# State-space branch stepped by four tokens with matrix powers, and the masks of a stick-breaking head issued as a group

## The chip, the cores and the metric

The kernel runs on one NeuronCore of one Trainium2 chip. The metric is the device time of one execution in microseconds (us). Engines: PE (TensorE, matrix products; PEld are its weight loads), DVE (VectorE), ACT (ScalarE), POOL (GpSimd), SP (SyncE, which here only issues DMAs).

## The reference, cut to what matters

Two transformer blocks follow each other on a sequence of 512 tokens (plus 256 context or memory tokens). The change is in the mixer of the second block, which has three branches on one projection: stick-breaking attention (8 heads of 64), a causal convolution, and a state-space model of 16 groups with 64 complex states each, 16 inputs and 16 outputs per group (1024 complex states in all). The first and the third are these:

```python
z = einsum('bhqd,bhkd->bhqk', qb, kh) * scale
mask = key_pos[None, :] < q_pos[:, None]
log_1mb = where(mask, log_sigmoid(-z), 0.0)
later = cumsum(log_1mb, axis=3, reverse=True) - log_1mb
w = where(mask, exp(log_sigmoid(z) + later), 0.0)
out = einsum('bhqk,bhkd->bhqd', w, vh)
...
# a = exp(lambda dt), |a| = mag;  b~ = f * b
bu = einsum('blgh,gph->blgp', u, bbr), einsum(..., bbi)
x[l] = a * x[l-1] + bu[l]              # complex, by an associative scan
y[l] = Re(c x[l]) + d * u[l]
o_ssm = (y @ glu_w)[:, :256] * sigmoid((y @ glu_w)[:, 256:])
```

The three branches are normed, joined and multiplied with the output weights (`w_out`).

## The kernel before, in words

Activations lie transposed: channels on the 128 partitions, tokens on the free axis. Every large product runs over a stream of 307 weight tiles of 128 x 1024 (`PLAN`; SP loads them into `RAW`, ACT rounds the high part into `HL`, POOL subtracts it for the low part, line 568, and PE multiplies three pairs). `T_OUT2` is the first tile of the second block's `w_out`, `T_U2` the first of its input projection. The order of the work is written out by hand, engine by engine; semaphores tie the engines together.

Between the last tile of the key and value projections of the memory and tile `T_OUT2` no weight tile is multiplied. This stretch, called the head loop here, is the stage that the change is in. PE first turns the state-space input weights (line 1194), multiplies the first half of the convolution's pointwise product (`conv_point(0)`, line 1142), then `state_in(0)` (line 1173), and then runs `stick(h)` for the eight heads:

- for the key blocks i = 3, 2, 1, 0 a score product (line 1209: 64 rows of the array, 128, 256, 384 and 512 columns) and behind each of them a mask product that adds a large negative value on the diagonal block (line 1210: 128 rows, 128 columns). ACT takes |z| of each bank (line 1822), then one exp and one ln over all four (lines 1825, 1827); DVE adds max(z, 0) (line 2759, tile `SPB`).
- meanwhile PE does `state_in(h + 1)` (2 products of 512 columns), then `values(h - 1)` of the head before (line 1235; in head 0 `conv_point(1)` stands here).
- the ten cumulative-sum products on `SPB` (line 1222), whose results ACT turns into weights (line 1833), and last `state_out(h - 1)` (line 1183, 2 products of 512 columns).

The eight state chunks c hold 128 complex states each. In `turn_in` DVE turns the input by the phase of each token within a 128-token segment (tables `TC`, `TS_`), `state` runs the scan with the real factor `mag`: four segments, one behind the other, with the last value turned and carried over (lines 2724, 2729, 2731), and `turn_out` (lines 2737 to 2741) turns back. `state_y` adds `d * u`. `discretize` (lines 2616 to 2622) multiplies the input weights with f before PE turns them. In head 0 ACT also rounds the first three `w_out` tiles (line 1368), and the third waits until POOL has freed a `RAW` buffer and SP has refilled it. Earlier, POOL makes the phase tables between the tiles from `T_TURNS` on (line 623). `PE`, `ACT`, `DVE` each follow their own list, so an instruction that waits holds all behind it on its engine.

After the heads the branches are normed (`mix_...`), the gated product is made (line 1261), and `w_out` starts (line 728).

## Time and profile before

| | us |
|---|---|
| median of 3 runs (2536.8 to 2538.82) | 2537.65 |
| the profiled execution, whole | 2538.42 |
| its span, first to last instruction | 2536.6 |
| head loop, first pointwise product to last values product | 1810.30 to 1944.13 |
| PE busy over the span | 2432.7 (96%) |
| DVE / ACT / POOL busy | 1420.1 / 912.8 / 1048.4 |

The page gives the busy time of each engine, forty slices of the span and the chain of work that ended last. Busy shares over the whole span say little on a stage of 134 us; the stage is read from the chain of waits, from the timeline (instructions in order of time) and from the busy times of chosen windows.

### The profile page before, as it was taken

The page shows a single profiled execution, that of the slowest core. Times are in us where ns is not written, and L with a number is a line of the kernel's source. Part 1 is how long each engine was busy: PE and PEld are TensorE (multiplying, and loading weights), DVE is VectorE, ACT ScalarE, POOL GpSimd, SP SyncE. Part 2 cuts the span into 40 slices and gives each one's busy share as a digit, 9 for nine tenths or more (in the row PEclk, how much of TensorE's full clock was granted, in tenths as well). Part 3 has the DMA queues.
Part 4 walks back from the last instruction along what each step waited for, and adds up shares of the span by engine and source line. Part 5 has one row for each costly group of instructions (what it writes and reads, how often), then busy time and mean ns, then how long its engine had stood idle before and what let it go on. Part 6 is the DMA issues. An engine that isn't in the chain of part 4 may idle for free.

```text
span 2536.6 us, 32104 instructions
## 1 busy us (share of the span) xinstructions
PE 2432.7 (96%) x12008; PEld 2063.8 (81%) x12008; DVE 1420.1 (56%) x2012; ACT 912.8 (36%) x1436; POOL 1048.4 (41%) x815
## 2 busy tenths in 40 slices
PE   6999889999999999999999999999899999999999
PEld 5899789999999998766788888778554766788887
DVE  7747866746465644889542123455788433543433
ACT  4222333313131224778542233345334343322322
POOL 1523132535344422298644467445400332344444
PEclk8999999999999999999999999999899999999999
DMA  6424012323333331411223322233200221232323
GB/s 245 147 100 141 27 58 79 138 100 117 117 108 117 105 111 43 123 39 44 79 84 99 100 92 86 89 108 108 100 1 1 67 67 50 83 100 92 100 91 108
DMA packets 68855, 232.24 MB, mean 92 GB/s; under 512 B 8048, under 2 KB 10992, under 8 KB 68592
## 3 DMA queue, kind: packets, MB, share of 16 engines
q1 hardware_dynamic: 68720, 230.35, 27.4%
q8 instruction: 95, 1.56, 0.3%
q14 instruction: 40, 0.33, 0.0%
HBM read 219.57 MB, written 2.10 MB: 87 GB/s over the span
## 4 chain that ended last, share of the span: by engine, by line
PE 76%; issue 7%; DVE 7%; POOL 6%; ACT 2%; DMA 1%; SPq 1%; POOLq 0%; DVEq 0%; ACTq 0%
PE PS L710 55%; PE PS L728 8%; POOL HL L568 4%; PE PS L751 2%; PE PS L1222 1%; POOL XR L610 1%; PE PS L1209 1%; DVE RD L2530 1%; POOL PL L610 1%; SPq L467 1%; PE PS L1325 1%; DMA EARLY<-adastream 1%; PE PS L1235 1%; DVE OG L2344 1%; PE PS L1173 1%
## 5 line engine op out<-in xcount | busy, mean ns | idle before, releaser
L568 POOL TENSOR_TENSOR HL<-RAW,HL 128x512 fp32r<-128x512 f32 x614 | 873.6, 1445 | 1361.8 <-ACT HL L1368 1361.6
L710 PE MATMUL PS<-HID,HL 128*128 128x384 f32 (+1 forms) x2832 | 562.1, 359 | 1.0 <-DVE HID L2086 1.0
L710 PE MATMUL PS<-HA,HL 128*128 128x512 f32 (+2 forms) x2592 | 553.1, 365 | 8.7 <-DVE VA L2453 2.3
L710 PEld LDWEIGHTS PS<-HID,HL 128*128 128x128 f32 x2832 | 509.5, 188 | 51.8 <-DVE HID L2086 1.4
L710 PE MATMUL PS<-HB,HL 128*128 128x512 f32 (+2 forms) x2592 | 538.7, 359 | 0.0
L710 PEld LDWEIGHTS PS<-HA,HL 128*128 128x128 f32 x2592 | 465.4, 189 | 74.2 <-issue 22.5
L710 PEld LDWEIGHTS PS<-HB,HL 128*128 128x128 f32 x2592 | 462.8, 188 | 50.6
L1368 ACT ACTIVATE HL<-RAW 128x1024 fp32r<-128x1024 f32 x307 | 323.2, 1053 | 476.0 <-PE PS L710 386.2
L2142 DVE CUSTOM_DVE_ANT_0 ADJ<-ADA,CB 128x1024 f32<-128x1024 f32 x160 | 262.3, 1640 | 12.0 <-DVE X L2062 5.2
L2062 DVE SCALAR_TENSOR_TENSOR X<-PS,MOD,X 128x256 f32<-128x256 f32 (+1 forms) x160 | 80.7, 546 | 288.7 <-PE PS L710 274.4
L2091 DVE TENSOR_TENSOR T<-T 128x768 f32<-128x768 f32 (+1 forms) x64 | 73.4, 1148 | 198.5 <-ACT T L1429 198.2
L728 PE MATMUL PS<-HA,HL 128*128 128x384 f32 (+1 forms) x576 | 126.9, 376 | 13.7 <-DVE HA L2032 6.2
L1429 ACT ACTIVATE T<-PS 128x384 f32<-128x384 f32 (+1 forms) x96 | 46.8, 522 | 241.0 <-PE PS L710 164.9
L728 PEld LDWEIGHTS PS<-HA,HL 128*128 128x128 f32 x576 | 107.3, 195 | 31.0 <-issue 10.8
L728 PE MATMUL PS<-HB,HL 128*128 128x384 f32 (+1 forms) x576 | 121.6, 367 | 6.5 <-DVE HB L2788 4.4
L728 PEld LDWEIGHTS PS<-HB,HL 128*128 128x128 f32 x576 | 105.4, 191 | 19.6 <-DVE HB L2788 4.8
L1385 ACT ACTIVATE T<-X 128x512 f32<-128x512 f32 (+2 forms) x64 | 43.6, 684 | 209.6 <-issue 73.5
L2060 DVE TENSOR_TENSOR X<-PS,X 128x512 f32<-128x512 f32 x40 | 27.7, 691 | 147.3 <-PE PS L710 135.3
L610 POOL TENSOR_TENSOR XR<-X,XR 128x512 fp32r<-128x512 f32 x64 | 81.6, 1292 | 24.6 <-ACT XR L1695 24.4
L2086 DVE TENSOR_TENSOR HID<-T,HID 128x768 fp32r<-128x768 f32 (+1 forms) x64 | 75.3, 1176 | 2.6 <-DVE T L2091 0.4
L2903 DVE RECIPROCAL T<-T 128x512 f32<-128x512 f32 x22 | 73.8, 3353 | 0.8
L2901 DVE TENSOR_SCALAR T<-T 128x512 f32<-128x512 f32 x22 | 10.4, 474 | 102.7 <-ACT T L1951 102.7
(409 smaller groups left out, 2647.1 us busy)
## 6 DMA issues: line engine op xcount, KB each, us to landing
RAW<-wstream SPq DMA_DIRECT2D x307, 512.0 KB, 3.4
ADA<-adastream SPq DMA_DIRECT2D x80, 512.0 KB, 3.4
EARLY<-adastream SPq DMA_DIRECT2D x16, 512.0 KB, 14.6
QB<-QH SPq DMA_DIRECT2D x32, 128.0 KB, 2.3
X<-x_in SPq DMA_DIRECT2D x8, 384.0 KB, 6.6
QC<-QL SPq DMA_DIRECT2D x16, 128.0 KB, 2.3
out<-X SPq DMA_DIRECT2D x8, 256.0 KB, 2.2
X<-mem SPq DMA_DIRECT2D x1, 1024.0 KB, 5.7
```

The lines of the kernel that those rows point to most:

```text
L568: a = pool.tensor_tensor(HL[:, t % RING, 1, half], RAW[:, t % RAW_RING, half], HL[:, t % RING, 0, half].bitcast(F32), ALU.subtract)
L610: pool.tensor_tensor(rest, full, high.bitcast(F32), ALU.subtract).then_inc(S("att_prob"), 1)
L710: mm = pe.matmul(PS[:, bk, 0:hi - lo], w[:, wp, k * P:(k + 1) * P], a[:, ap, lo:hi], start=(k == 0 and (wp, ap) == (0, 0)), stop=(k == nk ...
L728: mm = pe.matmul(PS[:, bk, 0:hi - lo], HL[:, tt % RING, wp, k * P:(k + 1) * P], a[:, ap, lo:hi], start=(k == order[0] and (wp, ap) == (0, 0)),
L751: mm = pe.matmul(PS[:, bk, 0:width], H(k)[:, ap, b * P:(b + 1) * P], HL[:, t % RING, wp, kk * width:(kk + 1) * width], start=(k == 0 and ( ...
L1368: act.activation(HL[:, t % RING, 0, :], RAW[:, t % RAW_RING, :], ACT.Copy).then_inc(S("w_hi"), 1)
L1429: a = act.activation(T1[:, j % 2, lo:hi], PS[:, bk, 0:hi - lo], ACT.Relu)
L2062: a = dve.scalar_tensor_tensor(X[:, m, p:q], src, MOD[:, gate[0], gate[1] * KC + m, c:c + 1], X[:, m, p:q], ALU.mult, ALU.add)
L2086: dve.tensor_tensor(HID[:, j, 1, lo:hi], T2[:, j % 2, lo:hi], HID[:, j, 0, lo:hi].bitcast(F32), ALU.subtract).then_inc(S("hid_ready"), 1)
L2091: dve.tensor_tensor(T2[:, j % 2, lo:hi], T1[:, j % 2, lo:hi], T1[:, j % 2, lo:hi], ALU.mult).then_inc(S("hid_v"), 1)
L2142: dve.tensor_tensor_reduce(ADJ[:, :], tile, CB[:, v, :], 1.0, 0.0, ALU.mult, ALU.add, dst).then_inc(S("ada_done"), 1)
L2903: dve.reciprocal(T1[:, j % 2, x], T1[:, j % 2, x]).then_inc(S("ffn_step"), 1)
```

## The change

The state-space branch steps by four tokens. Tokens are dealt into four streams: token 4j + i goes to stream i, column j. `UU` holds the streams one behind the other, and 16 DMAs per use put the 32 channels of a pair of groups from the four streams on one set of 128 partitions (`U4`). POOL multiplies the input weights with f and with a to the powers 0 to 3 (`power_products`, `power_sums`), and the output weights with the conjugate powers (`CP`); so one product of 128 rows takes in four tokens, and the scan runs over 128 steps with the factor `mag` to the fourth, in one piece for each chunk, with no carry. Four chunks share a bank: `state_in(g)`, `turn_in(g)`, `state(g)`, `turn_out(g)` and `state_out(g)` run for g = 0, 1 only. What the four tokens of a step owe each other comes from a new product, `lag_products`, copied by ACT (`KER`), laid out by 16 DMAs (`LAG`) and multiplied with `U4` in `state_out`. The result is copied out by ACT and dealt back by 16 DMAs for each g. `discretize` is gone. The masks of a head are issued behind its four scores. `STATE_IN`, `LAGS`, `STATE_OUT`, `STATE_Y` are `[0, 1], 2, [4, 6], 6`.

```diff
+MOVED = {"keys": 16 * 5 * KV_HEADS, "u4": 16 * (5 * KV_HEADS + 16), "lags": 16 * (5 * KV_HEADS + 32),
+         "y": [16 * (5 * KV_HEADS + 48), 16 * (5 * KV_HEADS + 64)]}
+T_POWERS = T_U2 - 5
...
-            load(SMALL[:, :], small, "small_in")
-            stretch(T_OUT1 + 8, T_U2 + 8)
-
-            sp.wait_ge(S("norm_scaled"), of_norm("2m", "scaled", KC))
-            load(X[:, :, 0:NCTX], ssm_b, "b_in")
-            stretch(T_U2 + 8, T_OUT2 + RING)
+            load(SMALL[:, :], small, "side_in")
+            stretch(T_OUT1 + 8, T_POWERS - 2)
...
+            sp.wait_ge(S("turns_ready"), 1)
+            load(SSM[:, :, :, :], ssm, "side_in")
+            stretch(T_POWERS - 2, T_OUT2 + 2)
             sp.wait_ge(S("tile_done"), T_OUT2)
-            load(CC[:, :, :, :], ssm_c, "c2_in")
-            stretch(T_OUT2 + RING, LAST_TILE)
+            by_group = U4[:, :, :].rearrange("p (g q) n -> p q g n", q=4)
+            for q in range(4):
+                for i in range(4):
+                    move(by_group[32 * i:32 * i + 32, q], UU[32 * q:32 * q + 32, :, i * P:(i + 1) * P], "moved")
+            stretch(T_OUT2 + 2, T_OUT2 + RING + 1)
+            sp.wait_ge(S("act_once"), ACT_ONCE["lag_out"])
+            by_group = LAG[:, :, :].rearrange("p (g q) n -> p q g n", q=4)
+            for q in range(4):
+                for i in range(4):
+                    move(by_group[32 * i:32 * i + 32, q, :, 32 * i:P], KER[32 * q:32 * q + 32, :, 0:P - 32 * i], "moved")
+            for g in range(2):
+                sp.wait_ge(S("y_out"), g + 1)
...
+                for q in range(4):
+                    for i in range(4):
+                        move(X[32 * q:32 * q + 32, 4 + 2 * g + i // 2, i % 2 * P:(i % 2 + 1) * P],
+                             X[32 * i:32 * i + 32, 2 * g + q // 2, q % 2 * P:(q % 2 + 1) * P], "moved")
+            stretch(T_OUT2 + RING + 1, LAST_TILE)
...
+            def each(i):
+                return prm(i).unsqueeze(2).to_broadcast([P, KC, 32])
+            def power_products(pr, pi, nr, ni, wr, wi):
+                tt(PW[:, 0], pi, each(wi), ALU.mult)
+                link(tt(PW[:, 1], pr, each(wi), ALU.mult))
+                tt(nr, pr, each(wr), ALU.mult)
+                link(tt(ni, pi, each(wr), ALU.mult))
+            def power_sums(nr, ni, conjugate=False):
+                tt(nr, nr, PW[:, 0], ALU.add if conjugate else ALU.subtract)
+                return tt(ni, ni, PW[:, 1], ALU.subtract if conjugate else ALU.add)
...
                 turn_sums(2 ** i)
                 low(T_TURNS + 2 * i + 1)
             pool.sem_inc(S("turns_ready"), 1)
-            lows(T_TURNS + 14, T_OUT2 + AHEAD)
+            lows(T_TURNS + 14, T_POWERS)
+            pool.wait_ge(S("norm_scaled"), of_norm("2m", "scaled", KC))
+            pool.wait_ge(S("side_in"), 48)
+            br, bi = SSM[:, 0], SSM[:, 1]
+            power_products(br, bi, br, bi, R_FR, R_FI)
+            low(T_POWERS)
+            link(power_sums(br, bi))
+            low(T_POWERS + 1)
+            before = br, bi
+            for n in range(4):
+                now = into_state(3 - n)
+                power_products(*before, *now, R_LR, R_AI)
+                low(T_POWERS + 2 + 2 * n)
+                a = power_sums(*now)
+                link(a)
+                low(T_POWERS + 3 + 2 * n)
+                before = now
...
+            pool.wait_ge(S("tile_done"), T_OUT2)
+            pool.memset(LAG[:, :, :], 0.0)
+            before = out_of_state(0)
+            pool.tensor_copy(before[0], SSM[:, 2])
+            link(tt(before[1], ZERO[:, 0:1].unsqueeze(2).to_broadcast([P, KC, 32]), SSM[:, 3], ALU.subtract))
+            for n in range(1, 4):
+                now = out_of_state(n)
+                power_products(*before, *now, R_LR, R_AI)
+                link(power_sums(*now, conjugate=True))
+                before = now
+            pool.sem_inc(S("powers"), 1)
...
+            def state_in(g):
+                if g == 0:
+                    pe.wait_ge(S("bt_ready"), 4)
+                    pe.wait_ge(S("moved"), MOVED["u4"])
+                else:
+                    pe.wait_ge(S("bu_read"), g)
+                for part in range(2):
+                    for c in range(4):
+                        mm = pe.matmul(PS[:, 4 + part, c * P:(c + 1) * P], BT[:, part, 4 * g + c, :], U4[:, 4 * g + c, :],
+                                       start=True, stop=True)
                 mm.then_inc(S("bu_done"), 1)
...
+            def lag_products():
+                pe.wait_ge(S("powers"), 2)
+                pe.wait_ge(S("hm_scaled"), len(HEADS2.jobs))
+                for g in range(2):
+                    for part in range(2):
+                        for q in range(4):
+                            mm = pe.matmul(PS[32 * q:32 * q + 32, 7, g * P:(g + 1) * P], SSM[:, part, 4 * g + q, :],
+                                           CP[:, part, 4 * g + q, :], start=(part == 0), stop=(part == 1))
+                mm.then_inc(S("pe_once"), 1)
+            def state_out(g):
+                pe.wait_ge(S("states"), g + 1)
+                if g == 0:
...
+                    pe.wait_ge(S("y_out"), g)
+                for q in range(4):
+                    c, o = 4 * g + q, q * P
+                    pe.matmul(PS[:, 7, o:o + P], LAG[:, c, :], U4[:, c, :], start=True, stop=True)
+                    for part in range(2):
+                        mm = pe.matmul(PS[:, 7, o + 1:o + P], CP[:, part, c, :], XX[:, part, o:o + P - 1], start=False,
+                                       stop=True, skip_group_check=True)
                 mm.then_inc(S("y_done"), 1)
             for g in range(4):
...
+                pe.wait_ge(S("powers"), 1)
+                pe.wait_ge(S("hm_scaled"), len(HEADS2.jobs) - 1)
                 if g >= 2:
                     pe.wait_ge(S("bt_ready"), g - 1)
...
                         pe.wait_ge(S("sb_weights"), 4 * h - i)
                     lo = i * P
                     pe.matmul(PS[:, i, lo:NX], KS[p, c, lo:lo + P], QS[p, c, lo:NX], start=True, stop=True)
-                    pe.matmul(PS[:, i, lo:lo + P], const(C_ID), const(C_MS), start=False, stop=True,
+                for i in (3, 2, 1, 0):
+                    pe.matmul(PS[:, i, i * P:(i + 1) * P], const(C_ID), const(C_MS), start=False, stop=True,
                               skip_group_check=True).then_inc(S("sb_logits"), 1)
-                if h + 1 < KC:
-                    state_in(h + 1)
+                if h in STATE_IN:
+                    state_in(STATE_IN.index(h))
                 if h == 0:
                     conv_point(1)
...
                 else:
                                        SPB[:, SB_OFF[j]:SB_OFF[j] + NX - j * P], start=False, stop=True,
                                        skip_group_check=True)
                     mm.then_inc(S("sb_args"), 1)
-                if h:
-                    state_out(h - 1)
+                if h == LAGS:
+                    lag_products()
+                if h in STATE_OUT:
+                    state_out(STATE_OUT.index(h))
...
-            pe.wait_ge(S("bu_read"), KC)
-            for k in range(5):
+            pe.wait_ge(S("bu_read"), 2)
+            for k in range(6):
                 mix_sum(k)
-            state_out(7)
-            mix_sum(5)
...
+                if h == LAGS:
+                    act.wait_ge(S("pe_once"), PE_ONCE["lag_sums"])
+                    act.activation(KER[:, :, :], PS[:, 7, 0:2 * P].rearrange("p (g n) -> p g n", n=P),
+                                   ACT.Copy).then_inc(S("act_once"), 1)
+                if h in STATE_OUT:
+                    g = STATE_OUT.index(h)
+                    act.wait_ge(S("y_done"), g + 1)
+                    act.activation(X[:, 2 * g:2 * g + 2, 0:NCTX], PS[:, 7, :].rearrange("p (a n) -> p a n", n=NCTX),
+                                   ACT.Copy).then_inc(S("y_out"), 1)
...
+            def turn_in(g):
+                dve.wait_ge(S("bu_done"), g + 1)
+                dve.tensor_tensor(DTM[:, :, :], PS[:, 4:6, :], table(TS_, g), ALU.mult)
+                link(dve.tensor_tensor(IN[:, :, :], PS[:, 4:6, :], table(TC, g), ALU.mult))
+                dve.sem_inc(S("bu_read"), 1)
...
+            def state(g):
+                for c in range(4):
+                    mag = prm(R_M4, 4 * g + c).to_broadcast([P, P])
+                    o = slice(c * P, (c + 1) * P)
+                    for i in range(2):
+                        a = mark(dve.tensor_tensor_scan(ZZ[:, i, o], mag, IN[:, i, o], 0.0, ALU.mult, ALU.add))
+                done(a)
+            def turn_out(g):
+                if g:
+                    dve.wait_ge(S("y_done"), g)
+                dve.tensor_tensor(DTM[:, :, :], ZZ[:, :, :], table(TS_, g), ALU.mult)
+                link(dve.tensor_tensor(XX[:, :, :], ZZ[:, :, :], table(TC, g), ALU.mult))
+                dve.tensor_tensor(XX[:, 0, :], XX[:, 0, :], DTM[:, 1, :], ALU.subtract)
+                dve.tensor_tensor(XX[:, 1, :], XX[:, 1, :], DTM[:, 0, :], ALU.add).then_inc(S("states"), 1)
+                dve.wait_ge(S("states"), g + 1)
+            def state_y(g):
+                dve.wait_ge(S("moved"), MOVED["y"][g])
+                half = [x.rearrange("p (a n) -> p a n", n=NCTX) for x in (YS[:, g, :], UU[:, g, :])]
+                dve.scalar_tensor_tensor(half[0], half[1], pc(PC["ssd"] + g), X[:, 4 + 2 * g:6 + 2 * g, 0:NCTX], ALU.mult,
+                                         ALU.add).then_inc(S("y_read"), 1)
             dve.wait_ge(S("turns_ready"), 1)
-            link(dve.tensor_scalar(prm(R_W7N), prm(R_W7S), -1.0, None, ALU.mult))
...
                     dve.wait_ge(S("sb_summed"), h)
                     dve.tensor_copy(QS[:, h // 2 - 1, :], PS[:, 6, :]).then_inc(S("sb_out"), 1)
-                if h + 1 < KC:
-                    turn_in(h + 1)
-                state(h)
-                if h == 4:
+                if h < 6:
+                    (turn_in, state, turn_out)[h % 3](h // 3)
+                if h == STATE_Y:
                     state_y(0)
```

PE's row in a head without state work (head 3; the names are the queries and keys `QS`, `KS`, the constants `CST`, weights `AB`, values `VS`, softplus `SPB`). Before:

```order
L1209 MATMUL PS<-QS,KS 128x128
L1210 MATMUL PS<-CST 128x128
L1209 MATMUL PS<-QS,KS 128x256
L1210 MATMUL PS<-CST 128x128
L1209 MATMUL PS<-QS,KS 128x384
L1210 MATMUL PS<-CST 128x128
L1209 MATMUL PS<-QS,KS 128x512
L1210 MATMUL PS<-CST 128x128
L1173 MATMUL PS<-UU,BT 128x512 x2
L1235 MATMUL PS<-AB,VS 64x128
```

And of the changed kernel, the same head:

```order
L1310 MATMUL PS<-QS,KS 128x128
L1310 MATMUL PS<-QS,KS 128x256
L1310 MATMUL PS<-QS,KS 128x384
L1310 MATMUL PS<-QS,KS 128x512
L1312 MATMUL PS<-CST 128x128 x4
L1339 MATMUL PS<-AB,VS 64x128
```

The four masks stand behind the four scores, and the two state products in front of the values are gone; line 1183's two behind the sums are gone too.

DVE's row ahead of the heads, from the scaling of the convolution to the first softplus (`BX` and `X` are `discretize`, `CH`, `CY` the convolution's activation). Before:

```order
L1993 SCALAR_TENSOR_TENSOR CY<-CY,HT_154 128x512 x2
L2650 COPY VM<-PS 128x512 x2
L2616 TENSOR_TENSOR BX<-X,PRM 128x512 x2
L2619 TENSOR_TENSOR X<-X,PRM 128x4x128 x2
L2621 TENSOR_TENSOR X<-X,BX 128x4x128
L2622 TENSOR_TENSOR X<-X,BX 128x4x128
L2679 TENSOR_SCALAR CH<-CH 128x2x512
L2680 RECIPROCAL CH<-CH 128x2x512
L2681 TENSOR_TENSOR CY<-CY,CH 128x1024
```

And of the changed kernel:

```order
L2103 SCALAR_TENSOR_TENSOR CY<-CY,HT_154 128x512 x2
L2744 COPY VM<-PS 128x512 x2
L2771 TENSOR_SCALAR CH<-CH 128x2x512
L2772 RECIPROCAL CH<-CH 128x2x512
L2773 TENSOR_TENSOR CY<-CY,CH 128x1024
```

The six instructions of `discretize` between the value copies and the activation are gone.

## Rows read from the trace of the kernel before

**Rows 1.** Windows: stretch, length, then busy us (instructions) by engine, PE clock, DMA.

```profile
1810.00:1817.00 7.00, 6.70 (x9) 2.62 (x9) 1.56 (x4) 0.00 (x0) 0.00 (x0) 0.55 0.01 4
...
1875.00:1890.00 15.00, 15.00 (x54) 7.90 (x53) 13.23 (x26) 6.16 (x11) 0.00 (x0) 1.00 0.00 0
...
1931.00:1935.00 4.00, 2.98 (x11) 1.25 (x10) 3.45 (x4) 3.14 (x3) 0.00 (x0) 1.00 0.00 0
```

**Rows 2.** Chain of waits, one whole head: start, length, engine, tile, line.

```profile
1882.26 0.42 PE PS L1209 x2
1882.68 0.42 PE PS L1210 x2
...
1885.40 1.05 PE PS L1209 x2
...
1886.87 1.72 PE PS L1173 x4
...
1890.88 4.61 PE PS L1222 x20
```

**Rows 3.** Timeline, the last head, ACT and DVE.

```profile
1931.72 0.60 ACT L1822 ACTIVATE AB<-PS 128x512 f32<-128x512 f32 x1 [0.98 <-PE PS L1210]
...
1935.06 1.68 DVE L2759 SCALAR_TENSOR_TENSOR SPB<-PS,AB 128x128 f32<-128x128 f32 x4 [0.58 <-ACT AB L1827]
```

**Rows 4.** Chain of waits, the last head and the tail.

```profile
1927.08 0.42 PE PS L1209 x2
...
1935.41 4.71 PE PS L1222 x20
1940.12 1.72 PE PS L1183 x4
1941.84 2.30 PE PS L1235 x8
...
1950.37 1.72 PE PS L1183 x4
```

**Rows 5.** Timeline ahead of the heads, DVE and ACT.

```profile
1797.05 1.16 ACT L1802 ACTIVATE CH<-CY 128x512 f32<-128x512 f32 x2
...
1801.65 0.69 DVE L2679 TENSOR_SCALAR CH<-CH 128x1024 f32<-128x1024 f32 x1
```

**Rows 6.** Chain of waits, start of the loop to the second head.

```profile
1810.30 3.75 PE PS L1142 x4
1814.05 2.92 PE PS L1173 x4
...
1824.72 1.05 ACT HL L1368
1825.84 2.51 POOL HL L568 x2
1828.37 3.13 DMA RAW<-wstream
```

**Rows 7.** Timeline, second head: PE, ACT and DVE.

```profile
1829.75 1.60 DVE L2712 TENSOR_TENSOR IN<-IN,DTM 128x512 f32<-128x512 f32 x1
...
1832.48 1.40 ACT L1833 ACTIVATE AB<-PS 128x128 f32<-128x128 f32 x4
...
1832.79 0.49 PE L1209 MATMUL PS<-QS,KS 64*128 64x128 f32 x2 [2.08 <-ACT AB L1833]
...
1837.93 2.07 PE L1209 MATMUL PS<-QS,KS 64*128 64x512 f32 x2
```

**Rows 8.** Timeline: POOL's table products; and a DVE row with POOL idle.

```profile
1543.91 0.74 POOL L623 TENSOR_TENSOR TS__158<-TS__158,PX 128x256 f32<-128x256 f32 x1
...
1819.58 0.69 DVE L2712 TENSOR_TENSOR IN<-IN,DTM 128x512 f32<-128x512 f32 x1
```

**Rows 9.** Groups of instructions of the whole span, products with 32 weight columns.

```profile
L673 PE MATMUL PS<-EARLY,CVW 128*32 128x128 f32 x192 | 9.2, 372 | 6.1 <-DMA EARLY<-adastream 6.1
```

**Rows 10.** DMA issues of the page: KB each, median us to landing.

```profile
QC<-QL SPq DMA_DIRECT2D x16, 128.0 KB, 2.3
```

More of the change, by code:

```diff
@@ L396, in block_program @@
         (R_DT, R_MAG, R_TH, R_COS, R_SIN, R_FR, R_FI, R_W0C, R_W7N, R_W7C, R_W7S, R_T0, R_T1, R_T2, R_T3, R_AR,
-         R_AI) = range(17)
+         R_AI, R_LR, R_M4) = range(19)
         def prm(i, c=None):
@@ L643, in turn_sums, with into_state, out_of_state @@
                 link(tt(prm(R_W7S), prm(R_T2), prm(R_T2), ALU.add))
+            def each(i):
[8 more added lines that the diff above has]
+                return tt(ni, ni, PW[:, 1], ALU.subtract if conjugate else ALU.add)
+            def into_state(i):
+                return [X[:, :, part * P + 32 * i:part * P + 32 * i + 32] for part in range(2)]
+            def out_of_state(i):
+                return [CP[:, part, :, 32 * i:32 * i + 32] for part in range(2)]
             pool.wait_ge(S("dve_once"), ONCE["prm_ready"])
@@ L1240, in _ @@
             for h in range(SB_HEADS):
-                if h == 0:
-                    state_in(0)
                 stick(h)
@@ L2667, in _ @@
             a.then_inc(S("cv_centered"), 1)
-            discretize(0)
             heads_scale(HEADS2, len(HEADS2.jobs) - 1)
@@ L2676, in _ @@
             value_copies(0)
-            discretize(1)
             dve.wait_ge(S("cv_exp"), 2)
@@ L3053, in ssm_arrays @@
             rows = slice(64 * (g % 2), 64 * (g % 2) + 64)
-            out[rows, i, g // 2, 16 * (g % 8):16 * (g % 8) + 16] = a[g]
+            out[rows, i, g // 2, 16 * (g % 2):16 * (g % 2) + 16] = a[g]
     return out
@@ L3092 @@
         "ropes": rope_tables(),
-        "ssm_b": ssm[:, 0:2].transpose(0, 2, 1, 3).reshape(P, KC, 2 * P).copy(),
-        "ssm_c": ssm[:, 2:4].copy(),
+        "ssm": ssm_arrays(x),
         "small": small_weights(x),
```

143 lines of the change are left out of this document (46 added, 97 removed).

## The prediction

> **What bounds the kernel now.** I read the chain of waits first, then the busy times by window, then the timeline at the places where the chain changes its form. In the head loop the chain is PE from one head to the next with no wait in it: scores and masks alternate, then come two state products (1.72), four values products, ten sums (4.61) [rows 2]. The window over a steady head has PE busy in all of its 15.00 us, DVE in 13.23, ACT in 6.16, at full clock [rows 1]. So PE sets the pace there, one head in 14.94 us: from 1882.26 to 1927.08 are three heads [rows 2, 4]. Three places differ. Ahead of the loop DVE's list is last: the reciprocal's input step starts at 1801.65, though ACT had its operand at 1798.21 [rows 5]. In head 0 the list ACT, POOL, DMA, ACT for the third output tile comes last [rows 6], and PE then waits 2.08 us [rows 7]. In the last head, which has no `state_in`, PE waits between values and sums for ACT and DVE: masks end, |z| runs 1931.72 to 1932.32, DVE starts at 1935.06 and the sums at 1935.41 [rows 3, 4]. That head shows what a head looks like when state work goes, and it is the core of this forecast.
>
> **What a product costs.** Two products of 512 columns take 1.72 us [rows 2], so 1.68 ns a column. A score of 128 columns should then take 0.22 and takes 0.42, one of 512 should take 0.86 and takes 1.05; a mask should take 0.22 and takes 0.42. Each carries 0.2 us whatever its length. The ten sums (2560 columns, 4.30) take 4.61 in one go and the four values (1280 columns, 2.15) take 2.30 [rows 2, 4]: behind their like, short products carry nothing. The scores use 64 rows of the array, the masks 128. I therefore charge the 0.2 to a change of form, not to a product. The Trainium skill, "TensorEngine Tiling (Array Packing)", section "Key Properties", says that a change of tiling mode drains the array, while a change of tile does not; by that rule grouping saves six of eight drains a head, and rows 2 agree as far as they go. No row here has two 64-row scores behind each other, so the other reading (0.2 for every product of 64 rows) stays as a rival.
>
> **A plain head, step by step.** Scores 2.15 and masks 0.86 with two changes of form are 3.4 us, where 4.61 stood (1882.26 to 1886.87, [rows 2]). But the first mask now comes only after all scores, at 2.15 + 0.2 + 0.2 + 0.22 = 2.8 us from the head's start. Four passes of ACT over these shapes, one behind the other, take 1.40 [rows 7], so |z| ends at about 4.25; in the last head it ended 5.24 after the start (1927.08 to 1932.32 [rows 3, 4]). From there to the first sum are 3.09 us (exp, ln, softplus), unchanged. The sums start at 7.34 instead of 8.33 and take 4.71 [rows 4]: a head of 12.1 us. PE has 3.4 + 2.3 = 5.7 us of work until then and waits 1.6. So ACT's list, no longer PE, sets the first part of a head, and what falls away from PE between masks and sums (1.72 in `state_in`, 1.2 in changes of form) brings not 2.9 but 1.0; the 1.72 of `state_out` comes off in full.
>
> **The sum over the loop**, in the profiled execution.
> 1. Start. `discretize` leaves DVE's list, so the reciprocal's chain starts 3.35 us earlier, at 1798.3, and the pointwise product at 1806.95. PE has been idle since the transposes and will be at half clock there as before (0.55 in the first window [rows 1]). At half clock: pointwise 3.4, scores 4.5, masks 1.9, then the last |z|, exp and ln. `state_in(0)` no longer stands ahead (2.92 [rows 6]). ln ends at 1820.3 instead of 1824.72; it would be 1818.6 if the clock rises during the scores. From there the list of the third tile is the same 8.07 us (1824.72 to 1832.79, [rows 6, 7]), so head 1 starts 4.4 earlier. Sums of head 0 end by 1825 to 1828, in time.
> 2. Heads 1 to 6: before 1832.79 to 1927.08, 94.3 us. Now six heads of 12.1 are 72.6. Head 1 was slow at half clock (a score of 512 columns took 2.07 against 1.05 [rows 2, 7]) after the wait of 2.08; the wait is about as long now and may or may not do so: +1.2, the middle of 0 and 2.4. The eight `state_in` products of 128 columns are 1.72 and fill the wait. The lag products: 16 with 32 weight columns, which took 9.2 us for 96 [rows 9], so 1.5; if each cost a whole product, 3.4; I take 1.7, as they are of the same form as those rows. `state_out`: 12 products of 128 columns, 2.6, twice; if each paid 0.2, 5.0; I take 2.6, since all are of 128 rows like the sums. Together 80.7, a gain of 13.6.
> 3. Last head to the end of its values: 17.05 before (1927.08 to 1944.14), now 7.34 + 4.71 + 2.3 = 14.4: 2.7.
> 4. Tail: `state_out(7)` (1.72 at 1950.37 [rows 4]) goes from between two norm sums; DVE and ACT are close behind, so of it 0.6.
> 5. Losses. POOL makes the output powers in heads 1 and 2: 20 products of 256 elements at 0.74 [rows 8], a fill and a copy, 16 us. While POOL works, a DVE instruction takes 1.60 where it takes 0.69 alone [rows 7, 8]; a softplus is on the path, so up to 0.9 for one or two heads: -1. The 30 input-power products (22 us) and 14 small ones stand between POOL's weight tiles in a stretch where it has slack; but some fall beside the norm of block two, which DVE carries: 0 to 3, I take 0.3.
> Sum: 4.4 + 13.6 + 2.7 + 0.6 - 1.3 = 20.0. 2538.42 - 20.0 = 2518.4; the median of the runs shown lies 0.8 under the profiled execution: 2517.6.
>
> Costed at nothing, with their cover: the turns and scans. DVE did them for one chunk in 11.6 us (13.23 less the softplus's 1.68 [rows 1, 3]); the same turns and eight scans now serve four chunks and are spread over three heads of 12.1, so DVE is free whenever a softplus comes. The 16 DMAs of `U4` start when the last projection tile is done and have some 15 us, until the masks of head 0 end; those of `LAG` start at the end of head 2 and have two heads; those of the result have one to two. One lands in 2.3 us [rows 10]; 16 behind each other would need to cost over 1 us apiece to be seen. Two loads of 1 MB are replaced by one of half that, in stretches where weights are ahead.
>
> **Rivals.**
> - A: the clock falls in the plain heads. PE waits 1.6 us in each. After 2.08 us of wait it fell [rows 7]; in the last head, where it waited 1.4 between values and sums, it did not (1.00 [rows 1]). 1.6 lies nearer the second. If it falls in three or four of the six, the sums run part of their 4.3 us at half clock, some 1.7 each: +5 to 6, 2523.
> - B: the 0.2 belongs to every 64-row product and every mask. Then the last mask is no earlier, |z| ends at 5.24 as before, a head is 13.1: +1.0 in seven heads, 2525.
> - C: the output powers are late. Head 1 starts at 1828.3, POOL's third tile ends 2.7 later and the tables 16 after that, at 1847; they are wanted at 1828.3 + 13.3 + 12.1 = 1853.7; if each of the 20 were lengthened by 0.5 us by DVE, PE would wait 4 us ahead of the lag products, with the scores of head 3 queued behind and ACT waiting for their masks, and the clock would follow: 2523.
> - D, slower: the clock falls in the first wait and stays down. Before, head 1 still ran its last score at half clock, 5.1 us after it had resumed (1832.79 to 1837.93 [rows 7]). At half clock a head is 4.5 + 1.9 + 4.5 + 8.9 = 19.8 us, 7.7 more than 12.1, and the gain is gone from the third such head on; six give +46: 2564. Against it: full clock was back by head 4 [rows 1], and the sums are dense work.
> - E: the start warms up early and nothing collides: 1.7 + 1.2 + 1.3 more: 2513.5.
>
> **Chances.** Forecast 0.50, A 0.18, B 0.09, C 0.09, E 0.10, D with anything else that outweighs 20 us 0.04. Within 0.2% (5.1 us, about what a measurement of this kernel can tell from no change) of 2537.65 would need three of A, B and C at once: 0.02, taken from them. So faster 0.94, same 0.02, slower 0.04. The range runs from E to past A, B and C: 2512 to 2527.
>
> **What would show it.** Right: heads 3 and 5 of 12.1 us from score to score; scores 2.2 to 2.4 and masks 0.9 to 1.1 as groups; a PE wait of 1.6 between values and sums, released by DVE's softplus; pointwise product at about 1807; values of the last head end near 1923; granted clock 1.00 in heads 2 to 7. Wrong: scores of 2.9 (B), clock under 0.9 in the heads (A, D), PE waiting ahead of the lag products for POOL (C), or a DMA as releaser of `state_in(0)` or `state_out(0)`.

## The result, and the profile after

The changed kernel took 2520.59 us (median of 4 runs, 2519.58 to 2521.97) where the kernel before took 2537.23 in the same comparison: ratio 0.9937, 95% interval 0.9925 to 0.9950. A second set of runs gave 2517.09 and 0.9927 (0.9913 to 0.9941). The forecast was 2517.6, range 2512 to 2527. Faster by 17 to 19 us, as forecast, and by about the amount; but the parts of that amount are not those of the forecast.

A plain head first. Chain of waits of the changed kernel, head 3 with the lag products ahead of it (start, length, engine, tile, line; line 1310 are the scores, 1312 the masks, 1324 the sums, 1268 the lag products):

```profile
1852.55 1.01 PE PS L1268 x32
1853.56 2.35 PE PS L1310 x8
1855.91 0.43 PE PS L1312 x2
...
1856.42 1.43 ACT AB L1923 x4
...
1857.88 1.28 ACT AB L1926
...
1859.18 1.28 ACT AB L1928
...
1860.58 0.30 DVE SPB L2833
...
1860.93 4.71 PE PS L1324 x20
```

The chain leaves PE after the first mask and runs through ACT and DVE; before it never left PE [rows 2]. From 1853.56 the next head starts at 1865.64, after 12.08 us. Windows of this head and of the last one, columns as in [rows 1], where PE was busy in all 15.00 us of a window of that length:

```profile
1853.49:1865.57 12.08, 10.45 (x49) 6.51 (x45) 4.84 (x8) 5.50 (x10) 0.00 (x0) 1.00 0.13 29
...
1907.17:1923.55 16.38, 14.50 (x54) 8.45 (x53) 1.68 (x4) 7.34 (x13) 0.00 (x0) 0.90 0.07 17
```

The start of the loop in the changed kernel, timeline of DVE, SP and PE (in brackets: idle before, and what ended it):

```profile
1800.00 0.69 DVE L2771 TENSOR_SCALAR CH<-CH 128x1024 f32<-128x1024 f32 x1 [1.57 <-ACT CH L1903]
...
1804.48 11.11 SPq L525 DMA_DIRECT2D U<-UU  x16
...
1808.64 1.96 PE L1224 MATMUL PS<-CY,SMALL 128*128 128x512 f32 x4 [1.86 <-issue]
...
1812.88 1.16 PE L1312 MATMUL PS<-CST 128*128 128x128 f32 x8
1816.97 3.65 PE L1257 MATMUL PS<-U,BT 128*128 128x128 f32 x16 [2.93 <-DMA U<-UU]
```

Two things differ from the forecast. The pointwise product takes 1.96 for the two products that took 3.75 [rows 6]: the clock had not fallen. And `state_in(0)` waits 2.93 us for the moves of `U4`: SP needs 11.11 us to issue sixteen of them, 0.70 each, and the last lands at 1816.83. That is a transfer as releaser of `state_in(0)`, which the prediction named as a sign against it.

Cut into stretches, the stage reads like this (us; `start` is from the end of the last transpose to the first score of head 1, `tail` from the last values product to the `w_out` product that waits 4.4 us for DVE's `HB`, `rest` from there to the last instruction). `median` is that of the runs, the other columns are from one profiled execution; the kernels are described below. The first two and the third and fourth are the same kernel twice.

| kernel | median | ahead | start | head 1 | heads 2-6 | last head | tail | rest |
|---|---|---|---|---|---|---|---|---|
| before | 2537.2 | 1804.2 | 28.6 | 19.7 | 74.6 | 17.1 | 31.4 | 561.1 |
| before_again | 2535.4 | 1804.3 | 27.0 | 18.1 | 74.6 | 17.1 | 31.4 | 561.1 |
| changed | 2520.6 | 1806.8 | 21.2 | 12.4 | 66.8 | 16.4 | 31.3 | 565.2 |
| after_again | 2517.1 | 1804.8 | 21.2 | 13.7 | 66.8 | 14.7 | 31.3 | 565.2 |
| e_masks_only | 2531.1 | 1802.1 | 26.6 | 17.0 | 70.9 | 18.2 | 31.4 | 565.5 |
| e_masks_apart | 2524.7 | 1802.4 | 22.3 | 17.9 | 71.5 | 15.4 | 31.3 | 561.2 |
| e_state_behind | 2518.5 | 1803.2 | 24.4 | 15.4 | 66.8 | 14.7 | 31.3 | 565.6 |
| e_tile_behind | 2512.3 | 1805.3 | 22.3 | 12.4 | 66.8 | 14.7 | 31.3 | 561.2 |
| e_discretize | 2524.2 | 1805.5 | 24.5 | 13.7 | 66.8 | 14.7 | 31.3 | 565.3 |
| e_straight | 2520.3 | 1805.5 | 20.9 | 12.4 | 66.8 | 16.4 | 30.7 | 565.7 |
| e_fill_only | 2513.1 | 1806.9 | 19.8 | 12.4 | 66.8 | 14.7 | 31.3 | 561.2 |
| e_tile_fill | 2508.8 | 1804.3 | 16.7 | 12.4 | 66.8 | 14.7 | 31.3 | 563.2 |
| e_before_fill | 2536.2 | 1801.9 | 25.2 | 19.7 | 74.6 | 17.1 | 31.3 | 565.2 |
| e_before_tile | 2538.4 | 1806.4 | 23.4 | 19.7 | 74.6 | 17.1 | 31.4 | 565.2 |

From the stage (start to tail) the first pair of profiles has 23.2 us, the second 20.5. In the first pair `ahead` and `rest` take 2.6 and 4.0 of it back, though `rest` is the same code in both and `ahead` differs only in POOL's input powers and two loads. I first asked whether the change does that.

### The profile page after: what moved, and what is told of

It is laid out like the page before. It is cut to its first block, busy times and chain, and to the rows that moved or that the text cites. A ratio compares the mean times of both kernels' runs of the same rounds, so it can differ in the third digit from the quotient of the medians.

```text
span 2520.0 us, 32191 instructions
## 1 busy us (share of the span) xinstructions
PE 2410.5 (96%) x12056; PEld 2069.8 (82%) x12056; DVE 1341.5 (53%) x1855; ACT 912.2 (36%) x1439; POOL 1087.3 (43%) x879
## 4 chain that ended last, share of the span: by engine, by line
PE 78%; DVE 7%; POOL 5%; issue 5%; ACT 3%; DMA 1%; SPq 1%; POOLq 0%; DVEq 0%; ACTq 0%
PE PS L792 57%; PE PS L810 8%; PE PS L833 3%; POOL HL L592 2%; PE PS L1324 2%; POOL XR L634 1%; DVE RD L2640 1%; POOL PL L634 1%; PE PS L1425 1%; SPq L474 1%; PE PS L1310 1%; DMA EARLY<-adastream 1%; DVE OG L2454 1%; DVE SM L2624 1%; PE PS L892 0%
## 5 line engine op out<-in xcount | busy, mean ns | idle before, releaser
L2252 DVE CUSTOM_DVE_ANT_0 ADJ<-ADA,CB 128x1024 f32<-128x1024 f32 x160 | 264.3, 1652 | 12.8 <-DVE X L2172 5.2
L810 PEld LDWEIGHTS PS<-HA,HL 128*128 128x128 f32 x576 | 106.8, 194 | 30.7 <-issue 10.3
L810 PEld LDWEIGHTS PS<-HB,HL 128*128 128x128 f32 x576 | 107.0, 193 | 19.7 <-DVE HB L2861 4.8
```

Source lines behind the costliest of these rows:

```text
L810: mm = pe.matmul(PS[:, bk, 0:hi - lo], HL[:, tt % RING, wp, k * P:(k + 1) * P], a[:, ap, lo:hi], start=(k == order[0] and (wp, ap) == (0, 0)),
L2252: dve.tensor_tensor_reduce(ADJ[:, :], tile, CB[:, v, :], 1.0, 0.0, ALU.mult, ALU.add, dst).then_inc(S("ada_done"), 1)
```

## The experiments

Ratios are to the kernel before on the same chip, with 95% intervals.

**before_again and after_again.** No edit.

> The kernel before, unchanged, profiled once more. In the two profiles so far, code that is the same in both kernels took 3.0 us longer in the changed kernel ahead of the stage (by 1776 us) and 3.9 us longer behind it, always where the granted clock fell to half in one and not in the other. Theory T1 (these falls come and go from execution to execution of the same kernel): this profile differs from the first one of the same kernel by 1 to 3 us at some of those places, with clock falls at other places. Rival T2 (the change brings them on, by shifting loads or waits): this profile agrees with the first within 0.3 us at every one of these places.

> The changed kernel, unchanged, profiled and timed once more: the base for the experiments. T1: the stage itself (from the transposes at about 1785 us to the start of the output projection) takes the same time within 1.5 us, and the 3.0 us ahead of it and the 3.9 us behind it come out otherwise. T2: both are again there within 0.3 us. Time 2520.5, ratio 0.9935.

Measured 2535.35 (one run) and 2517.09, 0.9927 (0.9913 to 0.9941). Both theories were half right. `ahead` differs by 2.0 us between two profiles of the changed kernel, and at 974 us in the program before_again is 2.6 us later relative to the first profile of the same kernel than at 917, with low clock for 6.8 us at 956.4 that the first profile didn't have: such falls come and go. But `rest` was 561 twice and 565 twice, as T2 said. Only the later kernels settle that: 565 stands beside three kernels with the old state branch, and 561 beside three with the new one. So the long `rest` doesn't belong to the change. A window of the changed kernel:

```profile
2093.00:2100.00 7.00, 6.09 (x10) 2.67 (x11) 0.61 (x3) 1.27 (x5) 0.00 (x0) 0.53 0.00 0
```

And the window at the same place of the program in the kernel before:

```profile
2113.40:2120.40 7.00, 6.08 (x20) 3.39 (x21) 1.46 (x5) 2.75 (x8) 0.00 (x0) 1.00 0.00 0
```

At half clock PE gets through 10 instructions instead of 20. Shortly ahead of both PE waits the same 1.9 us for DVE; in one kernel the clock then falls, in the other not. What decides it stays open.

**e_masks_only** (kernel before, this one part alone).

```diff
-                    pe.matmul(PS[:, i, lo:lo + P], const(C_ID), const(C_MS), start=False, stop=True,
+                for i in (3, 2, 1, 0):
+                    pe.matmul(PS[:, i, i * P:(i + 1) * P], const(C_ID), const(C_MS), start=False, stop=True,
```

> The kernel before with one part of the change alone: the four masks of a head as a group behind its four scores. Theory (PE sets that head, and each of six dropped changes of form is worth 0.2 us): heads 1 to 6 go from 15.0 to 13.8 us, the last head loses 1.0, in all -8 us: 2529. Rival (DVE, busy 13.2 of 15.0 us with the chunk's turns and scans, becomes the bound): heads of 14.3 to 14.6, in all -3: 2534.

Measured 2531.07, 0.9978 (0.9967 to 0.9989). Heads 2 to 6 take 13.8, 14.3, 14.0, 15.0 and 13.8: about 1.0 us less where PE still sets the pace, 0.5 in head 3, where PE waits 0.45 us for DVE's softplus, and nothing in head 5, where it waits 1.10. Windows of heads 5 and 2 of this kernel:

```profile
1887.82:1902.81 14.99, 13.89 (x53) 7.72 (x52) 14.42 (x31) 5.71 (x10) 0.00 (x0) 1.00 0.00 0
1845.68:1859.49 13.81, 13.81 (x53) 7.73 (x53) 12.83 (x25) 5.71 (x10) 0.00 (x0) 1.00 0.00 1
```

DVE was the next bound, busy 12.8 to 14.4 us of every head, so the grouping brought 3.6 us over heads 2 to 6 and not 6. Both theories hold, each in its heads. The last head, which was to lose 1.0, took 18.2 instead of 17.1: the grouped masks lengthened PE's wait ahead of the sums from 1.43 to 2.17 us, the clock then fell for 3.4, and the sums took 6.20 for 4.71. The 0.2 us belong to the change of form: the scores of the changed kernel take 2.35 in one go, their 2.15 of columns and one change, and from a head's first score to the end of its last mask it is 3.51 us where it was 4.68. Rival B falls. The Trainium skill ("TensorEngine Tiling (Array Packing)", section "Key Properties") says that a change of tiling mode drains the array. The trace agrees as far as the time goes, with 0.2 us for a change.

**e_masks_apart** (changed kernel, that part alone undone).

```diff
-                for i in (3, 2, 1, 0):
-                    pe.matmul(PS[:, i, i * P:(i + 1) * P], const(C_ID), const(C_MS), start=False, stop=True,
+                    pe.matmul(PS[:, i, lo:lo + P], const(C_ID), const(C_MS), start=False, stop=True,
```

> The changed kernel with score and mask alternating again, the rest as it is. Theory (ACT's list from the last mask on sets the head, so a mask that ends 1.0 later costs 1.0): heads 2, 3, 5 and 6 of 13.1 us, in all +7: 2527.5. Rival (something else sets the pace by now, so the order of the masks is worth nothing): heads of 12.1 us, 2520.5. The wait of PE between values and sums should shrink from 1.6 to 1.4, and head 7 may keep full clock.

Measured 2524.66, 0.9955 (0.9940 to 0.9970), 7.6 over after_again. Heads 3 and 5 take 13.03 instead of 12.08, so 4.7 in heads 2 to 6 and 0.7 in the last one. In head 1 the clock was low for 10.2 us (17.9 against 12.4 and 13.7), which is 4 to 5 us; such falls stand there in other kernels too (before, 10.2 us), so nothing shows that the masks bring it. And `rest` happened to be the short one. The theory holds for the heads; that the total also fits is partly luck.

**e_discretize.** The price of what was taken off DVE's list.

```diff
             value_copies(0)
...
+            for i in range(2):
+                a = dve.tensor_tensor(bx[i], b[1 - i], fi, ALU.mult)
+            link(a)
+            for i in range(2):
+                a = dve.tensor_tensor(b[i], b[i], fr, ALU.mult)
+            link(a)
+            dve.tensor_tensor(b[0], b[0], bx[0], ALU.subtract)
+            link(dve.tensor_tensor(b[1], b[1], bx[1], ALU.add))
             dve.wait_ge(S("cv_exp"), 2)
```

> The changed kernel with six more products of 128 x 512 elements on DVE behind the first value copies, on scratch, of the form of the old discretize(1), so that DVE's list ahead of the reciprocal is as long again as before. Theory of the prediction (this list sets the pointwise product): input step, reciprocal and pointwise product start 3.1 to 3.4 us later; at the start of head 1 at least 2.5 of it are left: 2520. Rival (head 0 hides it: the moves of U4 and the third tile are last anyway): pointwise 3.3 later, head 1 under 1 later, 2518.

Measured 2524.24, 0.9955 (0.9940 to 0.9971). The input step follows straight on the last of the six (`b` and `bx` are `HR2` and `SQ2`); DVE of this kernel:

```profile
1801.40 0.68 DVE L2780 TENSOR_TENSOR HR<-HR,SQ 128x512 f32<-128x512 f32 x1
1802.12 0.69 DVE L2782 TENSOR_SCALAR CH<-CH 128x1024 f32<-128x1024 f32 x1
```

And its PE at the pointwise product (the first three of its four instructions):

```profile
1810.76 2.90 PE L1224 MATMUL PS<-CY,SMALL 128*128 128x512 f32 x3 [5.24 <-issue]
```

The wait is 5.24 us where it was 1.86 and 2.63, and head 1 starts 24.5 us after the transposes instead of 21.2. So all of the 3.1 to 3.4 arrives, the term of the prediction (3.35) is right, and the rival falls. It isn't one list moved as a whole, though: after the long wait the clock is low for 6.8 us and the pointwise product takes 3.75, the moves of `U4` then cost PE no wait, and the third tile's list is last (PE waits 2.35 for it). That is the head 0 of the forecast, and the start of 24.5 is near its 24.1. The ratio lies 4.6 to 7.1 us above those of the changed kernel, the stage (151.0 against 148.1 and 147.6) only 2.9 to 3.3; the rest is not explained by this profile.

**e_state_behind.** The moves of `U4` off the path.

```diff
-                if h in STATE_IN:
-                    state_in(STATE_IN.index(h))
+                if h == 1:
+                    state_in(1)
                 if h == 0:
                     conv_point(1)
+                    state_in(0)
```

> The changed kernel with state_in(0) behind conv_point(1) instead of ahead of it. Theory M (the 16 moves of U4, issued at 0.70 us each by SP, are late by 0.7 to 2.9 us in head 0, and with the 1.7 of the products themselves they stand ahead of conv_point(1), its copy on DVE and the first softplus): PE no longer waits for the move, the sums of head 0 end 2 to 4 us earlier than 1824.6 and 1828.0 in the two profiles. But head 1 starts only 0 to 2 earlier, since in the second profile the list of the third output tile (ACT, POOL, DMA, ACT, until 1825.77) is last there: in all -1, 2516 to 2519. Rival (the moves cost nothing, PE waits in head 0 for something else that ends then): no change of the sums.

Measured 2518.5, 0.9929 (0.9915 to 0.9942): the same as the changed kernel. PE no longer waits for the move, but the sums ended 22.1 us after the transposes, where they had ended after 21.2 and 19.8: in this profile the clock was low for 13.7 us from 1804.8. And then the second list of the theory is last. PE of this kernel (of the scores of head 1, 1827.54, seven of eight):

```profile
1806.00 3.75 PE L1224 MATMUL PS<-CY,SMALL 128*128 128x512 f32 x4 [2.80 <-issue]
...
1820.76 4.50 PE L1325 MATMUL PS<-SPB,CST 128*128 128x128 f32 x20
1827.54 2.84 PE L1310 MATMUL PS<-QS,KS 64*128 64x128 f32 x7 [2.28 <-ACT AB L1935]
```

ACT has only just done the third tile's high part, for which it had waited 4.81 us:

```profile
1826.26 1.06 ACT L1469 ACTIVATE HL<-RAW 128x1024 fp32r<-128x1024 f32 x1 [4.81 <-DMA RAW<-wstream]
```

**e_tile_behind.** As above, and the third tile behind the weights of head 0.

```diff
-                    for k in range(AHEAD):
+                    for k in range(AHEAD - 1):
                         high(t + k)
...
+                if h == 0:
+                    high(t + AHEAD - 1)
```

> As e_state_behind, and besides ACT's high part of the third output tile behind the weights of head 0 instead of ahead of them. Theory (two lists are last in turn in head 0, the moves with state_in(0) and conv_point(1), and the third tile's; only with both away is the sums' end what counts): head 1 starts within 0.5 us of the end of head 0's sums, 3 to 4 us earlier than in the changed kernel: 2514.5, ratio to before about 0.991. Rival: the tile's high part, now behind, delays ACT's |z| of head 1 by up to 1 us plus what it still waits for its DMA, and the gain is 0 to 1.

Measured 2512.25, 0.9904 (0.9889 to 0.9919). Head 1 starts with the end of the sums, with no wait, and keeps full clock (12.44). Yet the low clock in head 0 (13.7 us again) kept the start at 22.3. Of the 3.7 us between its span and that of after_again, 4.0 are the short `rest`; the stage itself took 147.5 us against 147.6. A gain of this edit alone is not shown.

**e_straight.** The strided write of the gated values undone. The kernel leaves out the dealing into streams, so the tokens of the state branch come out in another order; it is for the timing alone.

```diff
-                in_order = UU[:, c, :].rearrange("p (j i) -> p i j", i=4)
-                value, factor = (x.rearrange("p (i j) -> p i j", i=4) for x in (PS[:, VALUE_BANK[c], :], GR[:, c, :]))
-                dve.scalar_tensor_tensor(in_order, value, -1.0, factor, ALU.mult, ALU.mult).then_inc(S("glu_out"), 1)
+                dve.scalar_tensor_tensor(UU[:, c, :], PS[:, VALUE_BANK[c], :], -1.0, GR[:, c, :], ALU.mult,
+                                         ALU.mult).then_inc(S("glu_out"), 1)
```

> The changed kernel with the gated values written straight instead of with stride 4 (so the tokens of this branch come out in another order). Theory (the 0.6 us that the tail should have brought are eaten by two strided writes of DVE, 1.06 against 0.69 us each, and the next steps are DVE's): output projection restarts 0.6 us earlier after the last values, 30.7 instead of 31.3 us. Rival (something else on ACT or PE is last): 31.3 as before.

Measured 2520.32 (one run). The tail took 30.70 us instead of 31.30. A wait of PE in it, in the changed kernel:

```profile
1945.68 1.65 PE L810 MATMUL PS<-HA,HL 128*128 128x512 f32 x6 [1.35 <-DVE HA L2861]
```

The same wait in e_straight:

```profile
1943.51 1.65 PE L810 MATMUL PS<-HA,HL 128*128 128x512 f32 x6 [0.75 <-DVE HA L2861]
```

That is the 0.6 of step 4, spent by two writes with a stride, 1.06 us each where a straight one takes 0.69.

**e_fill_only.** Does the clock make the spread of the start?

```diff
+            pe.wait_ge(S("cv_var_read"), 1)
+            keep_clock(5, 6)
             conv_point(0)
...
+                if h == 0:
+                    fill(h)
                 if h in STATE_IN:
...
+                if h == 7:
+                    fill(h)
                 for i in (3, 2, 1, 0):
                     pe.wait_ge(S("sb_softplus"), 4 * h + 4 - i)
...
+            def fill(h):
+                if h in (0, 7):
+                    keep_clock(3, 7 if h == 0 else 4)
```

`keep_clock(n, bank)` multiplies constants of 256 columns n times into a bank that nobody reads then.

> The changed kernel with products nobody reads in PE's waits: five of 256 columns ahead of the pointwise product, three in head 0 ahead of state_in(0), three in the last head ahead of the sums. Theory C (the start's spread, 17.2 to 19.6 us from the pointwise product to the end of head 0's sums, is the granted clock, which falls after PE's waits): full clock from 1800 to 1925 except perhaps around the wait for the moves of U4, which stay late; head 1 starts 18 to 19 us after the pointwise product, the last head takes 14.7 us instead of 16.4 where it fell: -1, 2517.5. Rival (the fill itself stands in the way of the work behind it): 1 to 2 us more than the changed kernel at the same points.

Measured 2513.11, 0.9912 (0.9896 to 0.9929). The clock is full from 1800 to 1949, through a wait of 1.81 us for the move, too; the start takes 19.8, the last head 14.7, the stage 145.0 against 147.6 and 148.1. The fill costs nothing in sight. Theory C holds. The median lies 4.4 us under the expected 2517.5; in its profile `rest` is 4.0 short, which isn't the fill's.

**e_tile_fill.** The edits of e_tile_behind and e_fill_only together; the fill of head 0 stands between `conv_point(1)` and `state_in(0)`.

> e_tile_behind (state_in(0) behind conv_point(1), high part of the third output tile behind the weights of head 0) with the same three fills. Theory: with neither the moves nor the third tile nor the clock in the way, ln of head 0 ends 8.8 us after the pointwise product and its sums 14 to 16 after it, head 1 starts at once: 3.5 to 5 us less than e_tile_behind, which had half clock all through head 0: 2508.5, the fastest kernel. Rival (ACT's list, not PE's clock, sets head 0): sums still end 19 us after the pointwise product, 2512.

Measured 2508.83, 0.9895 (0.9879 to 0.9912): the lowest median of all, though its interval still overlaps that of e_fill_only. Windows of this kernel, head 0 (from the pointwise product on) and head 1:

```profile
1806.30:1821.00 14.70, 14.60 (x67) 9.60 (x66) 7.86 (x12) 7.01 (x11) 4.84 (x4) 1.00 0.19 53
1821.06:1833.50 12.44, 12.24 (x62) 8.31 (x61) 6.05 (x10) 6.83 (x11) 10.51 (x15) 1.00 0.28 95
```

Head 0 took 19.3 and 18.5 us in the two profiles of the changed kernel and 14.7 here, with PE busy throughout. The stage takes 141.9. So three things held head 0 in turn (moves, third tile, clock). By single profiles of the stage, the moves taken away alone gave nothing (152.5, with half clock all through head 0), moves and third tile 0.1 (with the same half clock), the clock alone (with 1.7 of the last head in the larger figure) 2.7 to 3.1, all three 5.7 to 6.1. With the clock held, moves and third tile together are worth 3.1 (145.0 to 141.9).

**e_before_fill and e_before_tile.** Could the kernel before have had that as well? Thirteen fill products ahead of its pointwise product; in the second the third tile behind the weights, too.

```diff
+            pe.wait_ge(S("cv_var_read"), 1)
+            keep_clock(13, 6)
             conv_point(0)
```

> The kernel before with thirteen products nobody reads, of 256 columns, ahead of the pointwise product, where PE waits 6 us for DVE. This asks how much of the changed kernel's gain at the start was clock. Theory C: the fill holds full clock through head 0, where scores and masks take 4.7 us and conv products and state_in(1) 2.6; head 1 starts 2 to 4 us earlier after the pointwise product than the 22.5 and 21.1 of the two profiles: 2533. Rival (PE's clock doesn't count in head 0, ACT's and the third tile's lists are last): 21 to 22 us as before, 2536.

> The kernel before with the thirteen products nobody reads ahead of the pointwise product (as e_before_fill) and ACT's high part of the third output tile behind the weights of head 0. This asks whether the start's 6 to 7 us that e_tile_fill won belong to the change under study or could be had without it. Theory (they don't belong to it: the third tile's list makes PE wait 2.1 us ahead of head 1, the clock falls there, and head 1 takes 18 to 20 us instead of 15): head 1 starts 17.5 us after the pointwise product and takes 15.0 to 15.3, in all -6 to -7: 2529; the distance to e_tile_fill (2508.8) is then what the change itself brings, 20 to 21. Rival (without the changed kernel's shorter PE list the clock in head 1 stays low all the same): 2534.

Measured 2536.18, 1.0006 (0.9996 to 1.0016), for e_before_fill, and 2538.41, 1.0001 (0.9992 to 1.0010), for e_before_tile: nothing. The start shrinks from 28.6 and 27.0 to 25.2 and 23.4, as theory C has it, but the whole stage only from 171.3 and 168.2 to 168.0 and 166.1. In e_before_tile head 1 starts without a wait at full clock and has its masks after 4.68 us, and still takes 19.7. Its window:

```profile
1829.70:1849.40 19.70, 16.45 (x53) 8.83 (x52) 19.03 (x37) 7.48 (x12) 2.71 (x3) 0.91 0.32 116
```

DVE in the kernel before, timeline up to the softplus of head 1:

```profile
1839.57 1.22 DVE L2738 TENSOR_TENSOR XX<-ZZ,TC 128x1024 f32<-128x1024 f32 x1
1840.82 0.69 DVE L2739 TENSOR_TENSOR XX<-XX,DTM 128x512 f32<-128x512 f32 x1
1841.43 0.68 DVE L2741 SCALAR_TENSOR_TENSOR XX<-XX,DTM 128x512 f32<-128x512 f32 x1
1844.11 1.68 DVE L2759 SCALAR_TENSOR_TENSOR SPB<-PS,AB 128x128 f32<-128x128 f32 x4 [2.00 <-ACT AB L1827]
```

The same in e_before_tile, with one of its turns ahead:

```profile
1828.85 1.62 DVE L2716 TENSOR_TENSOR IN<-IN,DTM 128x512 f32<-128x512 f32 x1
...
1840.01 0.69 DVE L2743 TENSOR_TENSOR XX<-XX,DTM 128x512 f32<-128x512 f32 x1
1840.62 0.68 DVE L2745 SCALAR_TENSOR_TENSOR XX<-XX,DTM 128x512 f32<-128x512 f32 x1
1841.34 1.69 DVE L2763 SCALAR_TENSOR_TENSOR SPB<-PS,AB 128x128 f32<-128x128 f32 x4
```

In the kernel before, head 1 was at half clock and DVE still idled 2.0 us ahead of the softplus. In e_before_tile no idle is left: turns and scans of chunk 0 stand in a row behind the softplus of head 0, 15.0 us of work from 1826.35 on, and the softplus of head 1 behind them. 2.9 us of the 15.0 lie in three instructions (1.62, 1.17 and 1.83 us where their like take 0.69, 0.22 and 0.86) that run beside POOL's subtractions of weight tiles; without these the row would be some 12.1 long, near the 11.6 of a plain head. PE waits 3.25 us for the softplus, the clock falls there, and the sums take 6.08 us for 4.71. So with the clock held DVE is last, about as late as the clock had made it, and the rest is given back. Neither my theory nor my rival had DVE in it. This part of the gain does belong to the change: head 1 takes 12.4 because its state work is one step of three.

## Why the prediction was right, and where its sizes were not

Measured against the forecast's terms (4.4, 13.6, 2.7, 0.6 and a loss of 1.3), the two pairs of profiles give 7.4 and 5.9 us for the start, 15.0 and 12.2 for heads 1 to 6, 0.7 and 2.4 for the last head, 0.1 for the tail both times, and no loss that shows.

- **Plain head, step by step: right.** 12.08 for 12.1; scores 2.35; PE's wait ahead of the sums 1.64 for 1.6, released by DVE's softplus. Heads 2 to 6 took 66.8 for the forecast's 67.4 (five of 12.1, 1.7, two of 2.6). ACT's list sets the pace. One figure on the way is off: before, the sums of a head with `state_in` started 8.6 us after its first score (1882.26 to 1890.88 [rows 2]) and not 8.33, so 1.3 and not 1.0 comes off there; the 12.1 doesn't rest on it.
- **Step 1, start: mis-sized.** Forecast 24.1 us from the transposes to head 1 (1828.3 less 1804.2), measured 21.2. The step charged half clock "as before" to the pointwise product, scores and masks. But the edit itself shortened PE's wait ahead of them, from 6.1 us to 1.9 and 2.6, and the clock fell not at all or for 3.4 us. The prediction had the better case in hand ("1818.6 if the clock rises") and put it at 0.10 as rival E. Of E's second half, "nothing collides", the opposite came.
- **`U4` at nothing: failed.** The rows of the landing time [rows 10] were read, the issuing was not: sixteen issues on one queue take 0.70 us each, 11.1 in all, and 12.4 with the landing. At half clock (9.8 us from the pointwise product by the forecast) the masks would have ended 14 us after the start of the moves and hidden them, as they did in e_discretize, where the clock was low and PE didn't wait; at full clock they end after 9.6. The two errors hid each other. Price: 2.9 and 0.7 us of wait in the two profiles; in the second PE then waits 1.4 more for the third tile's list.
- **Step 2, head 1: right in size, half the cause.** The slow head 1 of before was put down to the clock [rows 7]. In that kernel the clock was last, since DVE idled 2.0 us; but e_before_tile shows DVE's list as a second bound, nearly as long. "DVE is free whenever a softplus comes" was true of after; that it was not so before was missed, so e_masks_only was over-expected as well.
- **Lag products:** 1.01 for 1.7. Of the three groups behind [rows 9] two ran at half clock (32 products in 3.64 us each) and one at full clock (1.96, or 1.0 for 16); the mean of 9.2 for 96 hid that. `state_out`: 2.7 twice for 2.6 (head 4, 14.76 against 12.08).
- **Step 3:** 14.7 for the last head where the clock held (forecast 14.4), 16.4 where it fell in the sums. That is the event of rival A, in one of the two profiles and only in the last head.
- **Step 4:** 0.06 for 0.6, because of the strided writes; they were in the diff and not costed.
- **Step 5:** POOL beside DVE cost nothing that shows. The softplus took 1.68 in head 1, with POOL busy in 11.8 of 12.4 us, as in the plain heads. The input powers: the code before the transposes took 1802 to 1807 us in all kernels, with old and new state branch at both ends, so no cost is seen, and one of a few us is not excluded.
- **Rivals.** C: the powers were ready at 1842.4, wanted at 1852.5. D: in the two profiles of the changed kernel no head ran at half clock throughout; at most 3.4 us of one were slow.
- **The rest.** The stage gave 23.2 and 20.5 for 20.0. That the total came out near the forecast is partly luck: the start gave more than its step, by the case that the sum had left to rival E, the losses of 1.3 didn't come, and 4 us of clock behind the stage, of which no step spoke, took back what was over.

## What to carry to other kernels

Count the issues of small moves as work of the queue that issues them, not only their landing. Where an edit shortens a wait of PE, work out the clock behind it anew, and then ask what the faster PE runs into. When one edit to a start shows nothing, list all chains that end within 2 us of each other before giving it up: here two or three had to go together. And compare kernels over the stage, with the code outside as a control: outside it the same code varied by 4 us.

## What the runs showed of the hardware

- Products of 32 weight columns into four different quarters of the output partitions overlap: 16 of 128 columns took 1.01 us in a row, where 16 times 128 columns at 1.68 ns would be 3.4. Four of their instructions, one for each quarter, start within 0.02 us, and the next four 0.11 us later.
- In the stage every wait of PE of 2.1 to 6.1 us, in all kernels, had a fall of the clock to half in it or close behind it, for 3.4 to 13.7 us. The waits of 1.4 to 1.6 us between values and sums in heads 2 to 6, five in each kernel with the new state branch, had none. Of 1.9 us both came: at the start of the loop the clock stayed up (changed kernel, and e_straight with 1.8), and in the last head it fell in two profiles (changed kernel, e_straight) and stayed up in four. One wait of 1.4 ahead of head 1 was followed by a fall too (after_again). Products that nobody reads, in the waits, kept it up from 1800 to 1946 in both kernels that had them in all three places.
- A POOL subtraction of 128x512 (weights) beside DVE went with a DVE product of 1.43 (changed kernel) and 1.62 us (e_before_tile) where its like took 0.69; POOL's products of 128x256 in head 1 left the softplus at 1.68.
- DVE's write of 128x512 gated values with a stride of four elements took 1.06 us, the straight one in e_straight 0.69.
